# Prompt attention of one inference step: the turn of a unit moved from two to three units behind its scores, with a third buffer of probabilities

## The chip, the core and the metric

The kernel runs on one core of one Trainium2 chip. The metric is the time of one execution on the device, in microseconds (us); of several runs the median is given. The core has a matrix engine (TensorE, PE in the profile), with its weight loads shown apart as PEld, a vector engine (VectorE, DVE), an activation engine (ScalarE, ACT), GpSimd (POOL) and SyncE (SP), which issues most of the DMA transfers. Each engine works through its own list of instructions in order; engines wait for each other with semaphores.

## What is computed

One layer of a hybrid decoder for a prompt of 1024 rows and for 8 samples of 4 rows that share its weights: an RG-LRU head group, an attention group with compressed, selected and window branches, and a feed-forward block. The change touches only the selected and the window branch of the prompt. Cut to what matters (8 heads of 64, 2 key heads, 4 query heads to each key head):

```python
def sel_attend(q, q_pos, idx, valid, kg, vg):      # selected: with 1024 rows, all 16 blocks of 64 keys up to the query
    s = jnp.einsum('bqkgd,bqknld->bqkgnl', qg, kg).astype(jnp.float32) * ATTN_SCALE
    s = jnp.where(m, s, NEG_INF).reshape(B, Sq, N_KV_HEADS, GROUP, n_sel * SEL_BLOCK)
    p = jax.nn.softmax(s, axis=-1).astype(q.dtype)
    o = jnp.einsum('bqkgm,bqkmd->bqkgd', p, vg.reshape(...))

def window_prompt(q, kv):                          # window: the last 512 keys, in blocks of 128 queries
    s = jnp.einsum('bnqkgd,bnskd->bnkgqs', qb, band[:, :, :, 0]).astype(jnp.float32) * ATTN_SCALE
    p = jax.nn.softmax(jnp.where(m, s, NEG_INF), axis=-1).astype(q.dtype)
    o = jnp.einsum('bnkgqs,bnskd->bnqkgd', p, band[:, :, :, 1])

attn = g[:, :, 0] * o_c + g[:, :, 1] * o_s + g[:, :, 2] * o_w     # the gates of the three branches
```

Everything is in float32. The new keys and values are outputs too, so the tile kvn that holds them is stored to memory.

## The kernel before

The stages follow one another as blocks: input projection with the recurrent group, keys and values, compression of the blocks of keys, prompt attention, sample attention, and the trunk with output projection and feed-forward. The block of the prompt attention is the function prompt_attention.

Its work is cut into N = 128 units, listed in `order`: for each of four passes i (KA = 4, a query head of each key head), for each of 8 query tiles t of 128 rows, for the branch br (1 selected, 2 window), for each key head h. So a pass has PER = 32 units, and a unit's number in its pass is u = 4t + 2(br - 1) + h. A unit attends to w key tiles of 128: t + 1 tiles in the selected branch, at most 5 in the window branch. What is done for unit n:

- qk(n), L1458 to L1481 on PE: scores into PSUM, in two products (L1475, L1477) for a high and a low part of the queries, and a mask product (L1480). Scores of odd and even units have halves of their own (place), so qk(n) waits for the exponential of n - 2.
- top(n), L1657 on DVE: the maximum of each row, once the scores are there.
- exp(n), L1562 on ACT: exponential out of PSUM into probs[n % 2], with the row sums (a second instruction that reads the accumulator).
- weigh(n), L1674 and L1675 on DVE: reciprocal of the sum, then probabilities times reciprocal and gate, in place.
- turn(n), on PE: transposes of each 128x128 tile of the probabilities, the first four into PSUM bank 4 (L1490), the others into bank 5 (L1497). It waits for weigh(n), for the copy of the unit before out of bank 4, and in its second half for the copy out of bank 5. Units with w over 4 (`second`) have a second half: those of tiles t = 4 to 7.
- copy(n), on ACT for bank 4 (L1570) and on DVE for bank 5 (L1666), into pT[n % 4].
- weighted(v), on PE: for the pair of units 2v and 2v + 1, which are the two key heads, the product of the transposed probabilities with the values (L1516), summed over both branches in one bank, behind the compressed branch's product (L1508). take(v) on ACT (L1578) copies the finished tile.

Each engine's order is written out by hand as a loop over the iteration n. PE: qk(n), turn(n - 2), at some u a piece of the compressed branch, and at even n weighted((n - 4) // 2). ACT: copy(n - 2), exp(n), pieces, at odd n a take. DVE: top(n), weigh(n - 1), copy(n - 2), pieces. These pieces belong to the next pass: the compressed branch's scores on PE at u = 3 (L1447), shifted on DVE at u = 4 (compress_shift, L1630 to L1634, and pick_gates, L1623), their exponential on ACT, weighing on DVE at u = 6, transposes on PE at u = 9 and their copy on DVE at u = 10; and the split of the queries into high and low part (stage, L1615 and L1618 on DVE, double, L1551 on ACT), one half at u = 19 for the next pass and the other at u = 3 for the running one.

Where buffers lie: probs[0] and probs[1] in `space`; pT[0] and pT[1] in kT, whose transposed keys are dead once split into KS; pT[2] and pT[3] in the columns of kvn that held the compressed branch's keys and values. kvn's columns 256 to 384 hold the selected keys, which the loop doesn't read, but which are an output. The stores of kvn's rows (semaphore kv_stored) are issued in the stage of keys and values; SP waits for them at the end of this block.

Of the kernel before, what the change touches and what calls it, by code (L numbers as in the profile page):

```python
# [27 lines left out]
ACT = mybir.ActivationFunctionType  # L28
# [4 lines left out]
P = 128  # L33
D_MODEL = 1024
SEQ = 1024
DEC_BATCH = 8
# [9 lines left out]
KV_WIDTH = N_KV * HEAD_DIM  # L46
# [19 lines left out]
TILES = SEQ // P  # L66
# [1237 lines left out]
def prompt_attention(k, q_plain, q_rot, qT, qR, kvn, kT, gates, ck_p, cv_p, attnT, attn_sum, ident, ones, kv_stored, scratch_stored,  # L1304
# [7 lines left out]
    nc, ps, psum, d = k.nc, k.ps, k.psum, k.dram  # L1312
# [8 lines left out]
    order = [(i, t, br, h) for i in range(KA) for t in range(TILES) for br in (1, 2) for h in range(N_KV)]  # L1321
# [16 lines left out]
    with ExitStack() as st:  # L1338
# [4 lines left out]
        def take_space(n):  # L1343
            nonlocal at
            at += n
            return space[:, at - n:at]
        cmask = take_space(TILES * NBP).rearrange("p (t n) -> p t n", t=TILES)
        vx = take_space(4 * P).rearrange("p (x n) -> p x n", x=4)
        probs = [take_space(SEQ), take_space(SEQ)]
        acc = take_space(SEQ)  # L1350
        diag, tail = probs[0][:, 0:P], probs[0][:, P:2 * P]
        flat_kT = kT[:, :, :].rearrange("p a n -> p (a n)")
        pT = [flat_kT[:, p * SEQ:(p + 1) * SEQ].rearrange("p (j n) -> p j n", j=TILES) for p in range(2)] + [
            kvn[:, 0:TILES, p * P:(p + 1) * P] for p in range(2)]
        own = [slice(h * HEAD_DIM, (h + 1) * HEAD_DIM) for h in range(N_KV)]
        KS = [sb(nc, st, f"k_halves{h}", [P, 2, SEQ], F32R) for h in range(N_KV)]
# [83 lines left out]
        def _(pe):  # L1440
# [43 lines left out]
            def turn(n):  # L1484
                pe.wait_ge(scaled, n + 1)
                w = len(tiles_of[n])
                if n >= 1:
                    pe.wait_ge(copied0, n)
                for j in range(min(w, 4)):
                    m = pe.transpose(ps[4][:, j * P:(j + 1) * P], probs[n % 2][:, j * P:(j + 1) * P], ident[:, :])  # L1490
                m.then_inc(turned0, 1)
                if second[n]:
                    if upto[n] >= 2:
                        pe.wait_ge(copied1, upto[n] - 1)
                    pe.wait_ge(cmp_copied, min(trip_of(n)[0] + 2, KA))
                    for j in range(4, w):
                        m = pe.transpose(ps[5][:, (j - 4) * P:(j - 3) * P], probs[n % 2][:, j * P:(j + 1) * P], ident[:, :])  # L1497
                    m.then_inc(turned1, 1)

            def weighted(v):  # L1500

                i, t, br, _ = order[2 * v]
                bank = ps[6 + t % 2]
                if br == 1:
                    if v >= 4:
                        pe.wait_ge(taken, (v // 2 - 1) * N_KV)
                    pe.wait_ge(cmp_copied, i + 1)
                    pe.matmul(bank[:, 0:P], lhsT=vx[:, t % 4, :], rhs=cT[i % 2][:, t // 4, :], start=True, stop=False, skip_group_check=True)  # L1508
                pe.wait_ge(copied0, 2 * v + 2)
                if second[2 * v + 1]:  # L1510
                    pe.wait_ge(copied1, upto[2 * v + 1])
                tiles = tiles_of[2 * v]
                for j, kt in enumerate(tiles):
                    for h in range(N_KV):
                        col = 2 * KV_WIDTH * br + KV_WIDTH + h * HEAD_DIM
                        m = pe.matmul(bank[own[h], 0:P], lhsT=kvn[:, kt, col:col + HEAD_DIM], rhs=pT[(2 * v + h) % 4][:, j, :],  # L1516
                                      start=False, stop=(br == 2 and j == len(tiles) - 1), skip_group_check=True)
                m.then_inc(out_summed, 1)
# [8 lines left out]
            for n in range(2, DONE):  # L1527
                i, u = trip_of(n)
                if n < N:
                    qk(n)  # L1530
                if 0 <= n - 2 < N:
                    turn(n - 2)
                if i + 1 < KA:
                    if u == CMP_AT:
                        compress_scores(i + 1)
                    if u == TURN_AT:
                        compress_turn(i + 1)
                if n % 2 == 0 and n >= 4:
                    weighted((n - 4) // 2)
            for t in range(TILES):  # L1540
                pe.wait_ge(squared, t + 1)
                m = pe.matmul(ps[4][:, 2 * t:2 * t + 2], lhsT=acc[:, t * P:(t + 1) * P], rhs=ones[:, 0:2], start=True, stop=True)
# [2 lines left out]
        @block.scalar  # L1545
        def _(act):
            def double(i, half):
                cols = slice(half * HQ, (half + 1) * HQ)
                for h in range(N_KV):
                    act.wait_ge(q_hi_done, (i * 2 + half) * N_KV + h + 1)  # L1550
                    act.activation(QD[h][own[1 - h], cols], QD[h][own[h], cols].bitcast(F32), ACT.Copy).then_inc(q_doubled, 1)  # L1551

            def exp(n):
                act.wait_ge(max_ready, n + 1)
                if n >= 2:
                    act.wait_ge(turned0, n - 1)
                    if second[n - 2]:
                        act.wait_ge(turned1, upto[n - 2])
                w = len(tiles_of[n]) * P
                if n >= 4:  # L1560
                    act.wait_ge(scaled, n - 3)
                act.activation(probs[n % 2][:, 0:w], psum[:, place[n]:place[n] + w], ACT.Exp,  # L1562
                               bias=nmax[:, n % 4:n % 4 + 1], accum_out=den[:, n % 4:n % 4 + 1]).then_inc(probs_ready, 1)

            def copy(n):
                act.wait_ge(turned0, n + 1)
                if n >= 4:
                    act.wait_ge(out_summed, (n - 4) // 2 + 1)
                w = min(len(tiles_of[n]), 4)
                act.activation(pT[n % 4][:, 0:w, :], ps[4][:, 0:w * P].rearrange("p (j n) -> p j n", j=w), ACT.Copy).then_inc(copied0, 1)  # L1570

            def take(v):

                i, t, _, _ = order[2 * v]
                act.wait_ge(out_summed, v + 1)
                for h in range(N_KV):
                    head = i + h * GROUP
                    act.activation(attnT[own[head % 2], head // 2, t * P:(t + 1) * P], ps[6 + t % 2][own[h], 0:P], ACT.Copy  # L1578
                                   ).then_inc(taken, 1)

            def compress_exp(i):
                act.wait_ge(cmp_shifted, i + 1)
                act.activation(cs[:, :, :, :], cs[:, :, :, :], ACT.Exp).then_inc(cmp_exp, 1)

            for h in range(N_KV):
                split_hi(act, KS[h][own[h], :, :], kT[own[h], :, 0:SEQ]).then_inc(k_hi_done, 1)
            double(0, 0)
            compress_exp(0)
            double(0, 1)
            for n in range(DONE + 1):  # L1590
                i, u = trip_of(n)
                if 0 <= n - 2 < N:
                    copy(n - 2)
                if n < N:
                    exp(n)
                if n < N and u == EXP_AT and i + 1 < KA:
                    compress_exp(i + 1)
                if n < N and u == FIRST_HALF_AT and i + 1 < KA:
                    double(i + 1, 0)
                if n < N and u == SECOND_HALF_AT and i:  # L1600
                    double(i, 1)
                if n % 2 == 1 and n >= 5 and order[n - 5][2] == 2:
                    take((n - 5) // 2)

        @block.vector
        def _(dve):
# [62 lines left out]
            def weigh(n):  # L1669
                i, t, br, h = order[n]  # L1670
                j = slice(n % 4, n % 4 + 1)
                w = len(tiles_of[n]) * P
                dve.wait_ge(probs_ready, n + 1)
                s.then(dve.reciprocal(coef[:, j], den[:, j]))  # L1674
                dve.tensor_scalar(probs[n % 2][:, 0:w], probs[n % 2][:, 0:w], coef[:, j], gsel[i % 2][:, t, br, h:h + 1],  # L1675
                                  ALU.mult, ALU.mult).then_inc(scaled, 1)

            s.then(dve.memset(ck_pair[:, :, :], 0.0))
# [18 lines left out]
            for n in range(1, DONE):  # L1697
                i, u = trip_of(n)
                if n < N:
                    top(n)  # L1700
                if n - 1 < N:
                    weigh(n - 1)
                if 0 <= n - 2 < N:
                    copy(n - 2)
                if i + 1 < KA:
                    if u == SHIFT_AT:
                        compress_shift(i + 1)
                        pick_gates(i + 1)
                    if u == PROBS_AT:
                        compress_weigh(i + 1)  # L1710
                    if u == COPY_AT:
                        compress_copy(i + 1)
                    if u == FIRST_HALF_AT:
                        stage(i + 1, 0)
                if 0 < i < KA and u == SECOND_HALF_AT:
                    stage(i, 1)
# [1258 lines left out]
```

## Time and profile before

| what | before |
|---|---|
| three runs | 1849.24, 1849.65, 1858.37 us; median 1849.65 |
| the profiled execution | 1851.05 us, of which the span of the page is 1849.3 us |
| PE busy | 1686.2 us (91%) |
| weight loads (PEld) busy | 1490.7 us (81%) |
| DVE busy | 946.8 us (51%) |
| ACT busy | 755.9 us (41%) |
| POOL busy | 333.2 us (18%) |
| the loop of the prompt attention | about 545 to 836 us |
| granted clock, mean over the span | 0.946 |

Times in rows are us from the start of the span. In a row of the timeline come start, duration, engine, line, operation, the tile written and those read, shapes, and in brackets the idle time of this engine before it, with the work that ended it. The page names tiles by the memory they lie in: probs and attnT are shown as hT, PSUM as banks, pT as kT or kvn. A stretch's row has for each engine the busy time and the count of instructions, then the granted PE clock (1 is 2.4 GHz, 0.5 is 1.2 GHz), the DMA share and GB/s.

### The profile page before, as it was taken

The numbers are of one execution on the slowest core, as the hardware profiler recorded it, in microseconds if no ns is written. First come the engines' busy times: TensorE is split into PE (matmuls) and PEld (weight loads), VectorE is DVE, ScalarE is ACT, GpSimd is POOL, SyncE is SP. The second block draws the span as 40 slices with busy tenths as digits, with TensorE's granted clock in tenths as the row PEclk, the third lists the DMA queues.
The fourth block names the chain that finished last, engine by engine and source line by source line (L and its number), as shares of the span: only waits on it lengthen the run. The fifth ranks groups of instructions, "written<-read, shape, count | busy, mean of one in ns | idle before, by whom it ended". The sixth has DMA issues, their size and how long they took to land. (4 is left out here: it accounts for less than half of the span.)

```text
span 1849.3 us, 29408 instructions
## 1 busy us (share of the span) xinstructions
PE 1686.2 (91%) x11059; PEld 1490.7 (81%) x11059; DVE 946.8 (51%) x1611; ACT 755.9 (41%) x1233; POOL 333.2 (18%) x359
## 2 busy tenths in 40 slices
PE   6999979889968888897679979999999999999998
PEld 3888945468856676674469979999999999999997
DVE  3747662335457777674466624443444443444433
ACT  3435501134436666661233435432335432355322
POOL 1100042411020010011036404004205014100032
PEclk7999989978869999998889989999999999999999
DMA  8345320155300000104534544444544545545443
GB/s 292 105 148 171 99 74 23 47 172 179 119 6 1 1 2 1 52 2 194 230 102 136 170 151 133 137 117 132 159 136 136 152 118 148 143 130 159 123 141 94
DMA packets 297019, 214.38 MB, mean 116 GB/s; under 512 B 20365, under 2 KB 284349, under 8 KB 293662
## 3 DMA queue, kind: packets, MB, share of 16 engines
q1 hardware_dynamic: 290268, 172.34, 31.7%
q0 software_dynamic: 4816, 40.73, 5.9%
q8 instruction: 60, 0.98, 0.2%
q10 hardware_dynamic: 1842, 0.05, 0.1%
q14 instruction: 33, 0.27, 0.0%
HBM read 205.81 MB, written 11.41 MB: 117 GB/s over the span
## 5 line engine op out<-in xcount | busy, mean ns | idle before, releaser
L423 DVE TENSOR_TENSOR ff_lo<-ff_raw,ff_hi 128x2048 fp32r<-128x2048 f32 (+1 forms) x126 | 267.1, 2120 | 213.3 <-ACT ff_hi L419 213.0
L428 PE MATMUL banks<-low_rows,ff_hi 128*128 128x352 f32 x1120 | 359.6, 321 | 0.0
L427 PE MATMUL banks<-ff_h_hi,ff_hi 128*128 128x352 f32 x1056 | 342.6, 324 | 12.5 <-DVE ff_lo L423 12.5
L429 PE MATMUL banks<-ff_h_hi,ff_lo 128*128 128x352 f32 x1056 | 339.2, 321 | 0.0
L419 ACT ACTIVATE ff_hi<-ff_raw 128x2048 fp32r<-128x2048 f32 (+1 forms) x126 | 215.4, 1710 | 230.9 <-PE banks L429 225.1
L428 PEld LDWEIGHTS banks<-low_rows,ff_hi 128*128 128x128 f32 x1120 | 211.5, 189 | 0.3
L427 PEld LDWEIGHTS banks<-ff_h_hi,ff_hi 128*128 128x128 f32 x1056 | 198.7, 188 | 13.7 <-issue 13.5
L429 PEld LDWEIGHTS banks<-ff_h_hi,ff_lo 128*128 128x128 f32 x1056 | 198.4, 188 | 0.0
L427 PE MATMUL banks<-hid_hi,ff_hi 128*128 128x352 f32 x528 | 171.9, 326 | 4.4 <-DVE hid_lo L423 4.1
L429 PE MATMUL banks<-hid_hi,ff_lo 128*128 128x352 f32 x528 | 169.9, 322 | 0.0
L428 PE MATMUL banks<-hid_lo,ff_hi 128*128 128x352 f32 x528 | 169.8, 322 | 0.0
L419 ACT ACTIVATE hid_hi<-streams 128x352 f32 (+1 forms) x66 | 32.9, 498 | 232.7 <-DVE streams L2629 232.7
L1657 DVE TENSOR_REDUCE neg_max<-banks 128x1 f32<-128x640 f32 (+7 forms) x128 | 90.2, 704 | 70.0 <-PE banks L1480 69.7
L1250 DVE COPY zt<-banks 64x256 f32<-64x256 f32 (+1 forms) x192 | 66.1, 344 | 81.0 <-PE banks L1195 77.8
L2629 DVE TENSOR_TENSOR streams<-streams,banks 128x352 f32<-128x352 f32 x66 | 34.4, 521 | 139.8 <-PE banks L429 139.7
L1490 PE MATMUL banks<-ident_m,hT 128*128 128x128 f32 x416 | 73.6, 291 | 34.7 <-DVE hT L1675 33.2
L427 PEld LDWEIGHTS banks<-hid_hi,ff_hi 128*128 128x128 f32 x528 | 99.6, 189 | 5.4 <-issue 3.7
L427 PE MATMUL banks<-h_hi,s_hi 128*128 128x352 f32 x288 | 101.8, 354 | 1.6 <-DVE h_lo L423 1.1
L1208 PE MATMUL banks<-zt,w 128*128 128x256 f32 (+1 forms) x384 | 97.3, 380 | 4.9 <-DVE zt L1250 4.1
L428 PEld LDWEIGHTS banks<-hid_lo,ff_hi 128*128 128x128 f32 x528 | 99.8, 189 | 0.0
L429 PEld LDWEIGHTS banks<-hid_hi,ff_lo 128*128 128x128 f32 x528 | 99.5, 188 | 0.0
L928 PE MATMUL banks<-w_nat,hT 128*128 128x396 f32 (+1 forms) x288 | 98.6, 502 | 0.0
(425 smaller groups left out, 3136.6 us busy)
## 6 DMA issues: line engine op xcount, KB each, us to landing
ff_raw<-in_w_gate SPq DMA_DIRECT2D x66, 512.0 KB, 3.9
ff_raw<-in_w_up SPq DMA_DIRECT2D x66, 512.0 KB, 5.1
ff_raw<-in_w_down SPq DMA_DIRECT2D x48, 384.0 KB, 3.9
late_ada<-in_w_ada SPq DMA_DIRECT2D x16, 1024.0 KB, 5.4
ff_raw<-in_w_down SPq DMA_DIRECT2D x48, 320.0 KB, 3.2
ff_raw<-in_w_out SPq DMA_DIRECT2D x24, 512.0 KB, 4.7
s_raw<-in_w_in SPq DMA_DIRECT2D x48, 128.0 KB, 2.4
streams<-in_x_prompt SPq DMA_DIRECT2D x4, 1024.0 KB, 8.9
```

What stands on the lines that cost most here:

```text
L419: return act.activation(hi, raw, ACT.Copy)
L423: return dve.tensor_tensor(lo, raw, hi.bitcast(F32), ALU.subtract)
L427: pe.matmul(out, lhsT=w_hi, rhs=x_hi, start=first, stop=False)
L428: pe.matmul(out, lhsT=w_hi, rhs=x_lo, start=False, stop=False)
L429: return pe.matmul(out, lhsT=w_lo, rhs=x_hi, start=False, stop=last)
L928: m = pe.matmul(ps[2 * (t % 2) + h][0:n, 0:HN], lhsT=hT[:, c, t * P:t * P + n], rhs=w[:, c, h * HN:(h + 1) * HN], start=(c == 0), stop=(c ...
L1208: m = pe.matmul(sums(g, c), lhsT=w1[p][:, c, l, :], rhs=zt[at % 2][:, c, 0:n], start=False, stop=False, skip_group_check=True)
L1250: copy(zt[at % 2][e * HEAD_DIM:(e + 1) * HEAD_DIM, :, h * n:(h + 1) * n], ps[4 + 2 * (at % 2) + e][h * HEAD_DIM:(h + 1) * HEAD_DIM, 0:2 * ...
L1490: m = pe.transpose(ps[4][:, j * P:(j + 1) * P], probs[n % 2][:, j * P:(j + 1) * P], ident[:, :])
L1657: dve.tensor_reduce(nmax[:, n % 4:n % 4 + 1], psum[:, place[n]:place[n] + w], AX, ALU.max, negate=True).then_inc(max_ready, 1)
L2629: dve.tensor_tensor(silu[p], silu[p], ps[2 * (1 - p) + 1][:, 0:GR], ALU.mult).then_inc(mixed, 1)
```

## The change

The turn of a unit comes one unit later, and what hangs on it too. A third buffer of probabilities takes the first 1024 columns of kT; the turned probabilities that lay there go to kvn's columns 256 to 384. On PE, turn(n - 3) stands behind qk(n), and weighted((n - 5) // 2) behind it at odd n. On ACT and DVE copy(n - 3) takes the place of copy(n - 2); exp(n) waits for the turn of n - 3 instead of n - 2; take moves on by one iteration. As the turned probabilities of unit 0 now overwrite selected keys of kvn, copy(0) on ACT waits until kvn is stored. DVE's order of top(n), weigh(n - 1) and the pieces stays. The whole diff:

```diff
--- before.py
+++ after.py
@@ -1346,11 +1346,11 @@
             return space[:, at - n:at]
         cmask = take_space(TILES * NBP).rearrange("p (t n) -> p t n", t=TILES)
         vx = take_space(4 * P).rearrange("p (x n) -> p x n", x=4)
-        probs = [take_space(SEQ), take_space(SEQ)]
+        flat_kT = kT[:, :, :].rearrange("p a n -> p (a n)")
+        probs = [take_space(SEQ), take_space(SEQ), flat_kT[:, 0:SEQ]]
         acc = take_space(SEQ)
         diag, tail = probs[0][:, 0:P], probs[0][:, P:2 * P]
-        flat_kT = kT[:, :, :].rearrange("p a n -> p (a n)")
-        pT = [flat_kT[:, p * SEQ:(p + 1) * SEQ].rearrange("p (j n) -> p j n", j=TILES) for p in range(2)] + [
+        pT = [kvn[:, 0:TILES, 2 * KV_WIDTH:2 * KV_WIDTH + P], flat_kT[:, SEQ:2 * SEQ].rearrange("p (j n) -> p j n", j=TILES)] + [
             kvn[:, 0:TILES, p * P:(p + 1) * P] for p in range(2)]
         own = [slice(h * HEAD_DIM, (h + 1) * HEAD_DIM) for h in range(N_KV)]
         KS = [sb(nc, st, f"k_halves{h}", [P, 2, SEQ], F32R) for h in range(N_KV)]
@@ -1487,14 +1487,14 @@
                 if n >= 1:
                     pe.wait_ge(copied0, n)
                 for j in range(min(w, 4)):
-                    m = pe.transpose(ps[4][:, j * P:(j + 1) * P], probs[n % 2][:, j * P:(j + 1) * P], ident[:, :])
+                    m = pe.transpose(ps[4][:, j * P:(j + 1) * P], probs[n % 3][:, j * P:(j + 1) * P], ident[:, :])
                 m.then_inc(turned0, 1)
                 if second[n]:
                     if upto[n] >= 2:
                         pe.wait_ge(copied1, upto[n] - 1)
                     pe.wait_ge(cmp_copied, min(trip_of(n)[0] + 2, KA))
                     for j in range(4, w):
-                        m = pe.transpose(ps[5][:, (j - 4) * P:(j - 3) * P], probs[n % 2][:, j * P:(j + 1) * P], ident[:, :])
+                        m = pe.transpose(ps[5][:, (j - 4) * P:(j - 3) * P], probs[n % 3][:, j * P:(j + 1) * P], ident[:, :])
                     m.then_inc(turned1, 1)
 
             def weighted(v):
@@ -1528,15 +1528,15 @@
                 i, u = trip_of(n)
                 if n < N:
                     qk(n)
-                if 0 <= n - 2 < N:
-                    turn(n - 2)
+                if 0 <= n - 3 < N:
+                    turn(n - 3)
                 if i + 1 < KA:
                     if u == CMP_AT:
                         compress_scores(i + 1)
                     if u == TURN_AT:
                         compress_turn(i + 1)
-                if n % 2 == 0 and n >= 4:
-                    weighted((n - 4) // 2)
+                if n % 2 == 1 and n >= 5:
+                    weighted((n - 5) // 2)
             for t in range(TILES):
                 pe.wait_ge(squared, t + 1)
                 m = pe.matmul(ps[4][:, 2 * t:2 * t + 2], lhsT=acc[:, t * P:(t + 1) * P], rhs=ones[:, 0:2], start=True, stop=True)
@@ -1552,18 +1552,20 @@
 
             def exp(n):
                 act.wait_ge(max_ready, n + 1)
-                if n >= 2:
-                    act.wait_ge(turned0, n - 1)
-                    if second[n - 2]:
-                        act.wait_ge(turned1, upto[n - 2])
+                if n >= 3:
+                    act.wait_ge(turned0, n - 2)
+                    if second[n - 3]:
+                        act.wait_ge(turned1, upto[n - 3])
                 w = len(tiles_of[n]) * P
                 if n >= 4:
                     act.wait_ge(scaled, n - 3)
-                act.activation(probs[n % 2][:, 0:w], psum[:, place[n]:place[n] + w], ACT.Exp,
+                act.activation(probs[n % 3][:, 0:w], psum[:, place[n]:place[n] + w], ACT.Exp,
                                bias=nmax[:, n % 4:n % 4 + 1], accum_out=den[:, n % 4:n % 4 + 1]).then_inc(probs_ready, 1)
 
             def copy(n):
                 act.wait_ge(turned0, n + 1)
+                if n == 0:
+                    act.wait_ge(kv_stored, 16 * (4 + DEC_BATCH))
                 if n >= 4:
                     act.wait_ge(out_summed, (n - 4) // 2 + 1)
                 w = min(len(tiles_of[n]), 4)
@@ -1589,8 +1591,8 @@
             double(0, 1)
             for n in range(DONE + 1):
                 i, u = trip_of(n)
-                if 0 <= n - 2 < N:
-                    copy(n - 2)
+                if 0 <= n - 3 < N:
+                    copy(n - 3)
                 if n < N:
                     exp(n)
                 if n < N and u == EXP_AT and i + 1 < KA:
@@ -1599,8 +1601,8 @@
                     double(i + 1, 0)
                 if n < N and u == SECOND_HALF_AT and i:
                     double(i, 1)
-                if n % 2 == 1 and n >= 5 and order[n - 5][2] == 2:
-                    take((n - 5) // 2)
+                if n % 2 == 0 and n >= 6 and order[n - 6][2] == 2:
+                    take((n - 6) // 2)
 
         @block.vector
         def _(dve):
@@ -1672,7 +1674,7 @@
                 w = len(tiles_of[n]) * P
                 dve.wait_ge(probs_ready, n + 1)
                 s.then(dve.reciprocal(coef[:, j], den[:, j]))
-                dve.tensor_scalar(probs[n % 2][:, 0:w], probs[n % 2][:, 0:w], coef[:, j], gsel[i % 2][:, t, br, h:h + 1],
+                dve.tensor_scalar(probs[n % 3][:, 0:w], probs[n % 3][:, 0:w], coef[:, j], gsel[i % 2][:, t, br, h:h + 1],
                                   ALU.mult, ALU.mult).then_inc(scaled, 1)
 
             s.then(dve.memset(ck_pair[:, :, :], 0.0))
@@ -1700,8 +1702,8 @@
                     top(n)
                 if n - 1 < N:
                     weigh(n - 1)
-                if 0 <= n - 2 < N:
-                    copy(n - 2)
+                if 0 <= n - 3 < N:
+                    copy(n - 3)
                 if i + 1 < KA:
                     if u == SHIFT_AT:
                         compress_shift(i + 1)
```

## Rows read from the trace of the kernel before

**Rows 1.** The page, busy time of each engine over the span

```profile
PE 1686.2 (91%) x11059; PEld 1490.7 (81%) x11059; DVE 946.8 (51%) x1611; ACT 755.9 (41%) x1233; POOL 333.2 (18%) x359
```

**Rows 2.** Busy time by stretch, the second and the fourth pass

```profile
618.00:690.00 72.00, 63.12 (x561) 49.77 (x561) 54.09 (x132) 46.38 (x117) 9.66 (x21) 0.95 0.00 1
...
763.00:836.00 73.00, 64.31 (x586) 50.22 (x582) 48.86 (x116) 45.06 (x114) 12.89 (x28) 0.95 0.10 34
```

**Rows 3.** Waits, 545 to 840: who waited for whom, us in total, times, longest

```profile
PEld banks L1490 <- DVE hT L1675: 42.8, 59, 2.1
...
PEld banks L1475 <- ACT hT L1562: 2.2, 10, 0.3
...
PEld banks L1497 <- DVE kT L1666: 0.7, 4, 0.2
```

**Rows 4.** Timeline, second pass, tiles t = 2 and 3

```profile
635.78 0.31 PEld L1490 LDWEIGHTS banks<-ident_m,hT 128*128 128x128 f32 x3 [0.42 <-DVE hT L1675]
...
641.85 0.69 ACT L1562 ACTIVATE hT<-banks,neg_max 128x512 f32<-128x512 f32 x1
...
643.21 0.60 ACT L1570 ACTIVATE kT<-banks 128x512 f32<-128x512 f32 x1 [0.59 <-PE banks L1490]
...
646.15 0.42 PEld L1490 LDWEIGHTS banks<-ident_m,hT 128*128 128x128 f32 x4 [0.48 <-DVE hT L1675]
```

**Rows 5.** Timeline, second pass, first wait of t = 4, then tile t = 7

```profile
650.55 0.42 PEld L1490 LDWEIGHTS banks<-ident_m,hT 128*128 128x128 f32 x4 [0.55 <-DVE hT L1675]
...
680.02 0.61 PE L1490 MATMUL banks<-ident_m,hT 128*128 128x128 f32 x4
680.22 1.23 DVE L1657 TENSOR_REDUCE neg_max<-banks 128x1 f32<-128x1024 f32 x1 [1.48 <-PE banks L1480]
...
680.49 0.39 PE L1475 MATMUL banks<-k_halves,q_doubled 128*128 128x320 f32 x1
...
682.28 0.28 DVE L1666 COPY kvn<-banks 128x128 f32<-128x128 f32 x1
682.42 0.42 PEld L1490 LDWEIGHTS banks<-ident_m,hT 128*128 128x128 f32 x4 [1.04 <-DVE hT L1675]
...
682.48 0.82 DVE L1657 TENSOR_REDUCE neg_max<-banks 128x1 f32<-128x640 f32 x1
...
683.40 0.81 DVE L1675 TENSOR_SCALAR hT<-hT,coef,gate_pair 128x1024 f32<-128x1024 f32 x1
...
684.69 0.41 PE L1475 MATMUL banks<-k_halves,q_doubled 128*128 128x320 f32 x1
...
685.57 0.60 PE L1490 MATMUL banks<-ident_m,hT 128*128 128x128 f32 x4
...
687.37 0.42 PEld L1490 LDWEIGHTS banks<-ident_m,hT 128*128 128x128 f32 x4 [0.58 <-DVE hT L1675]
```

**Rows 6.** Timeline, second pass, tiles t = 0 and 1

```profile
619.32 0.14 PEld L1490 LDWEIGHTS banks<-ident_m,hT 128*128 128x128 f32 x1 [0.47 <-DVE hT L1675]
...
621.35 1.87 PE L1447 MATMUL banks<-ck_pair,streams 128*128 128x32 f32 x16
...
625.49 0.14 PEld L1490 LDWEIGHTS banks<-ident_m,hT 128*128 128x128 f32 x1 [0.80 <-DVE hT L1675]
...
627.10 0.42 DVE L1657 TENSOR_REDUCE neg_max<-banks 128x1 f32<-128x256 f32 x1
...
628.10 0.29 PEld L1490 LDWEIGHTS banks<-ident_m,hT 128*128 128x128 f32 x2 [2.11 <-DVE hT L1675]
```

**Rows 7.** Timeline, second pass, split of the next queries at u = 19

```profile
655.01 0.86 DVE L1615 TENSOR_SCALAR q_doubled<-streams 64x512 fp32r<-64x512 f32 x2
...
657.34 0.96 DVE L1657 TENSOR_REDUCE neg_max<-banks 128x1 f32<-128x768 f32 x1
...
659.28 0.42 PEld L1490 LDWEIGHTS banks<-ident_m,hT 128*128 128x128 f32 x4 [1.27 <-DVE hT L1675]
```

**Rows 8.** Busy time by stretch, behind the longest wait of the second pass

```profile
627.90:634.70 6.80, 6.60 (x32) 4.66 (x33) 4.30 (x16) 3.40 (x13) 1.38 (x3) 0.51 0.00 0
```

## What the change was expected to do

> **What bounds the kernel now.** I read the page first: TensorE (PE) is busy 1686.2 of 1849.3 us [rows 1]. The change touches only the block of the prompt attention, so the next view is busy time by stretch. The block's loop runs from about 545 to 836 us in four passes of 73 us, one for each head pair. In the second, 618 to 690, PE is busy 63.1 of 72 us, VectorE (DVE) 54.1 and ScalarE (ACT) 46.4; the others look the same [rows 2]. So PE is nearest to a bound, with some 9 us idle in each pass, and what can be won here is that idle time, some 36 us in four passes, 2% of the kernel. The view of waits says whose it is: the weight loads of the transposes at L1490 stand 42.8 us idle for the weighed probabilities (L1675), while Q, the scores, wait for an exponential 2.2 us, and the second transposes (L1497) for the copy of their bank 0.7 us [rows 3]. One wait is nearly all of it.
>
> I write Q(n) for the scores of unit n, M for its maximum, E for its exponential, W for reciprocal and weighing, T and T1 for the transposes into bank 4 and bank 5, C (ACT) and C1 (DVE) for the copies out of these, V for the weighted sum of a pair. A unit's number u is within its pass; t = u // 4 is its query tile.
>
> The timeline shows the wait's form. V stands behind every second T. Where it stands between T(n-1) and T(n), W(n) has time. Where it doesn't, PE has one T and one Q of work, while DVE must do M(n+1) first and W(n) after it, since its queue has them in that order. At t = 7 M(29) starts at 680.22 and takes 1.23, so T(28) waits 1.04 us until 682.42 [rows 5]. PE's own row beside it shows 0.90; the 0.14 between them is the overlap of one instruction with the next that a wait costs as well, so I count in weight-load idle. In the second pass there are four such waits at t = 2 and 3, from 0.42 to 0.48, in sum 2.1 us [rows 4]; eight at t = 4 to 7, from 0.55 to 0.58, in sum 5.4 us [rows 5], of which the longest, 1.27 us, is where DVE splits the next half of queries [rows 7]; and at t = 0 and 1 two of 0.80 and 2.11 us around the compressed branch's scores [rows 6], and one of 0.47. That is 10.9 a pass; 42.8 / 4 = 10.7 agrees.
>
> **The change part by part.** No instruction is added or dropped, and the shapes are the same; moving one turn buffer to the dead selected keys costs nothing by the rows, as copies into either place (kT or kvn) take 0.60 us at 512 columns; the one into kT is in [rows 4].
>
> *The wait on W.* T(n-3) behind Q(n) needs W(n-3), which DVE finished a unit earlier. All 42.8 us of this wait go. What is late next is worked out for each part of a pass.
>
> *The second bank.* T1(n-3) needs C1(n-4), and C1(n-4) stands on DVE behind M(n-1) and W(n-2). Before, the wait in T for W hid this, since C1 follows directly behind W. Take the gap without a V that begins at the end of Q(30). DVE: M 0.82 starts 0.03 later; from 682.48 to the end of W at 684.21 it takes 1.73, a one-tile C1 (0.28, starting 0.08 before W's end) 0.20 more, and PE starts 0.06 after: 2.0 us. PE: T and T1 of five tiles 0.47 (680.02 to 680.49), starting 0.17 before Q's end, Q(31) 0.88 (684.69 to 685.57), four transposes 0.4 (by the five in 0.47): 1.6 us [rows 5]. So T1(28) waits some 0.4 us where T(28) waited 1.04. In the same way, from the same kinds of rows: T1(20) 0.2, T1(22) 0.4, T1(24) 0.25, T1(26) 0.45, T1(30) 0.3, where wider units lengthen M, W and C1 as much as Q. At the stage at u = 19 it is worse: DVE does M(19), W(18), C1(16), then the split of 2.3 us (655.01 to 657.34), M(20), W(19), and only then C1(17), at 6.0 us from the end of Q(19) [rows 7]; PE comes to T1(18) at 4.0, as it has T, V, Q, T, Q, T of work until then: 2.0 us of wait, where T(19) waited 1.27. With 0.14 for each of seven waits that makes 5.0 us instead of 5.4 in passes 0 to 2: nearly the whole gain of t = 4 to 7 turns into another wait, and 0.4 is left. The last pass has no such stage: 2.8 instead of some 4.2, 1.4 won. Sum 2.6 us.
>
> *Tiles 2 and 3.* No second bank there, so the 2.1 us go, unless ACT takes over: a pair at t = 3 costs it two C of 0.60, two E of 0.69 and 0.2 each, about 2.9 us with half a take [rows 4], against PE's 3.0; at t = 2 both stand at 2.3. I leave 0.4 for that: 1.7 a pass, 6.8 us.
>
> *Tiles 0 and 1.* The compressed scores take PE 1.87 us (L1447), and DVE shifts them ahead of M(5), which starts at 627.10, and T(4) waits for W(4) until 628.10 [rows 6]. After the change T(4) is a step later, but Q(7) stands in front of it, and needs E(5), ready at 628.1 too. So PE stops there still, some 2.0 us. What is won: V of the last pair (1.3 us) moves behind the compressed scores, where PE would only run towards this stop, less T(4) and V of the next pair (0.9) that come behind it, and 0.5 as DVE's split is over before M(4): 0.9, with the wait of 0.5 that goes, 1.4 us. I take 0.6 in pass 0, which has no last pair, and 1.4 in the others: 4.8 us.
>
> *The added wait*, kv_stored in C(0) on ACT: all of exp and copy would queue behind it. The passes show a DMA share of 0.00 to 0.01 and 1 GB/s [rows 2], so no such store is open then: nothing. The later last iteration costs nothing on PE, the work in it being the same: 0 to 0.5 us.
>
> *Sum:* 2.6 + 6.8 + 4.8 = 14.2 us, say 14.5 with rounding of the small waits. The profiled execution took 1851.05 us for a span of 1849.3; less 14.5 is 1836.6. The median shown is 1.4 below the profiled one, so 1835.2 us.
>
> **The clock, unknown in both directions.** In passes 1 to 3 the granted clock falls to 1.2 GHz for some 6.8 us behind the stop at t = 1; in 627.9 to 634.7 PE is busy 6.60 of 6.80 us [rows 8]. At 2.4 GHz this is 3.3 us of work: up to 3.3 a pass, 10 us, if the fall doesn't come. My stop of 2.0 is no longer one of two (0.80, then 2.11) but alone; against it there is a new stop of 2.0 at the stage at u = 19, where 1.27 brought no fall. I set one against the other and take 0. The Trainium skill ("TensorE: Matmul & The Clock Gate", section "HAM oscillation — how this bites in real kernels") has it that idle gaps throw the array back to the low clock and that dense work keeps it warm; by that alone the change would gain the 10 us as well. The trace agrees that the falls stand behind the longest stops, but some of these stay.
>
> **The rivals.**
> 1. *Forecast* (0.50): turn's wait goes, C1's takes half its place; 1835, own range 1828 to 1842.
> 2. *All of it is won* (0.20): DVE, freed of nothing but order, brings C1 in time, as 0.7 us of such waits in the trace now would suggest, and the stops at t = 1 shrink: 14.5 + 17 of C1's waits (3 x 5.0 + 2.8) = 32: 1818; or the clock stays up with my other terms, 10 more: 1825. Against it: DVE's order of M, W, C1 is fixed.
> 3. *It does hardly what it says* (0.20): the stop at the stage throws the clock down in three passes, 3.3 us each; 14.5 - 10 = 4.5: 1845. Or ACT is the bound at t = 1 to 3, and 7 us fall away.
> 4. *Slower* (0.10): W(n-1) waits for E(n-1), because ACT does the three-steps-old C first, which waits for T behind Q. Then M, W and C1 all shift, and each of the 28 gaps without V at t = 4 to 7 costs 1 us more: +28 - 14.5 = +13.5: 1863. It decides from the point where E(n-1) ends later than M(n). After the end of Q(n-1), E comes behind 0.3 of T, a C of 0.60 and its own 0.8 and 0.2 [rows 4, 5], so it ends at some 2.1; M(n) ends at some 3.1 even where no V lies between (T, T1 and Q 1.35, then DVE's C1 and M behind its own queue): 1 us short of it.
>
> **How the numbers follow.** A measurement of this kernel tells about 0.5%, 9.2 us, from no change: faster is under 1840.4. Forecast: 0.42 of its 0.50 under it; rival 2 wholly: 0.62. Same: 0.08, rival 3 with 0.18 and a little of 4: 0.29. Slower 0.09. The range holds the forecast, most of 2 and of 3: 1820 to 1848.
>
> **What would show it.** In the profile of the changed kernel L1490's wait for L1675 is near zero; L1497's wait for L1666 is 10 to 18 us with the longest, about 2 us, where the queries are split; Q at L1475 waits for L1562 about 2 us in each pass at t = 1; a pass takes about 69.5 instead of 73 us. If the waits at L1497 are small, rival 2 holds; if the clock is low after the stage, rival 3; if L1674 waits for L1562 in every unit, rival 4. The prediction is wrong, too, if the block after this one gives the time back, which reads nothing of it but its end.

## The result

The kernel after the change takes 1837.8 us (median of seven runs, 1829.3 to 1839.1) against 1850.0 us (seven runs, 1849.2 to 1858.4): a ratio of the means of 0.992, 95% interval 0.9898 to 0.9941. (Ratios here are of means; by the medians the gain is 12.2 us, by the means 14.8.) The forecast was 1835.2 us, with 1820 to 1848 as its range. The profiled execution took 1836.37 us for a span of 1834.1; the one before had 1849.3, so 15.2 us are gone from the span.

First the waits, 545 to 840 us of the kernel before in [rows 3], here 540 to 832 of the kernel after (columns: who waited for whom, us in total, times, longest). Lines have moved by two: weighing is L1677, the copies L1572 (ACT) and L1668 (DVE).

```profile
PEld banks L1497 <- DVE kT L1668: 9.3, 12, 1.6
...
PE banks L1490 <- ACT kvn L1572: 4.8, 5, 1.9
PEld banks L1497 <- DVE kvn L1668: 4.3, 12, 0.4
PEld banks L1475 <- ACT hT L1562: 3.8, 11, 1.1
PEld banks L1490 <- DVE hT L1677: 3.8, 5, 1.9
...
PEld banks L1490 <- DVE kT L1677: 2.5, 2, 2.1
```

Turn's wait for the weighing was 42.8 us in 59 places. Now 6.3 us are put down to it, in seven places, and the PE rows put 4.8 us of turn's waits down to ACT's copy out of bank 4; and the second transposes, L1497, wait 9.3 + 4.3 = 13.6 us in 24 places for the copy of their bank, where they waited 0.7. The place at u = 19, 1.27 us before [rows 7], shows it whole (timeline of after, DVE and PEld):

```profile
649.91 0.86 DVE L1617 TENSOR_SCALAR q_doubled<-streams 64x512 fp32r<-64x512 f32 x2
650.80 1.41 DVE L1620 SCALAR_TENSOR_TENSOR q_lo<-streams,q_doubled 64x512 fp32r<-64x512 f32 x2
652.24 0.96 DVE L1659 TENSOR_REDUCE neg_max<-banks 128x1 f32<-128x768 f32 x1
653.22 0.16 DVE L1676 RECIPROCAL coef<-den 128x1 f32<-128x1 f32 x1
653.42 0.61 DVE L1677 TENSOR_SCALAR hT<-hT,coef,gate_pair 128x640 f32<-128x640 f32 x1
653.95 0.29 DVE L1668 COPY kT<-banks 128x128 f32<-128x128 f32 x1
...
652.23 0.42 PEld L1490 LDWEIGHTS banks<-ident_m,kT 128*128 128x128 f32 x4 [0.33 <-issue]
654.29 0.14 PEld L1497 LDWEIGHTS banks<-ident_m,kT 128*128 128x128 f32 x1 [1.64 <-DVE kT L1668]
```

The first four transposes of unit 18 run at 652.23; the fifth waits until 654.29, 0.05 us behind the copy that frees its bank, and this copy of 0.29 us stands behind a split of 2.3 us, a maximum and a weighing that have nothing to do with it.

Where the time went, by tiles. Differences of the starts of the scores in the two timelines give, in us for each pass:

| | t = 0, 1 | t = 2, 3 | t = 4 to 7 |
|---|---|---|---|
| before, passes 0 to 3 | 17.7, 16.8, 16.0, 15.1 | 14.1, 14.6, 15.9, 14.2 | 41.4, 41.5, 41.4, 49.7 |
| after | 18.0, 15.6, 16.5, 12.9 | 13.6, 15.0, 13.4, 11.6 | 39.8, 39.8, 39.8, 47.8 |
| won | 2.6 | 5.1 | 6.8 |

The last value of each row of t = 4 to 7 reaches to the sums at the block's end. That is 14.4 us in all; the block also begins 0.6 us earlier; what follows the block takes 1010.5 us after and 1010.7 before. The tiles at t = 4 to 7, second pass, once more as stretches, before and then after (columns as in [rows 2]):

```profile
644.92:686.37 41.45, 37.24 (x353) 30.27 (x352) 32.22 (x66) 27.28 (x59) 5.52 (x12) 1.00 0.01 2
```

```profile
641.75:681.52 39.77, 37.11 (x348) 29.51 (x346) 31.96 (x66) 27.81 (x60) 6.32 (x12) 1.00 0.01 2
```

PE, DVE and ACT are as busy as before at the same clock; only idle time went, some 1.6 us of the 4.2 that PE had.

The clock has a part in the rest. In the profiled execution after, the low stretch behind the stop at t = 1 is still there in the second and third pass, but no longer in the last. These are t = 0 to 3 of the second and last pass, after:

```profile
611.16:641.75 30.59, 27.19 (x222) 20.65 (x220) 22.05 (x68) 18.60 (x58) 2.66 (x6) 0.89 0.00 1
...
751.25:775.75 24.50, 22.62 (x204) 16.71 (x203) 18.77 (x56) 18.08 (x57) 3.73 (x8) 1.00 0.26 98
```

The last pass, whose t = 0 to 3 took 29.3 us before at a granted clock of 0.88, takes 24.5 at 1.00. The first pass pays for it: the low stretch in which the loop begins ends at 556.1 us before and at 562.3 after. The stretch from 556 to 562 us, before and then after:

```profile
556.00:562.00 6.00, 4.17 (x34) 2.91 (x34) 4.74 (x18) 3.88 (x14) 0.00 (x0) 0.99 0.00 1
```

```profile
556.00:562.00 6.00, 6.00 (x29) 4.29 (x31) 4.89 (x17) 3.95 (x14) 0.00 (x0) 0.50 0.00 1
```

Within the block the stretches at 1.2 GHz add up to 36.1 us in either trace. So the clock by itself explains nothing of the 14.4 us; it took from the first pass what it gave to the last.

### The profile page after: what moved, and what is told of

Same layout as the page of the kernel before. It is cut to its first block and busy times, and to the rows that moved or that the text cites. A ratio compares the mean times of both kernels' runs of the same rounds, so it can differ in the third digit from the quotient of the medians.

```text
span 1834.1 us, 29407 instructions
## 1 busy us (share of the span) xinstructions
PE 1692.5 (92%) x11059; PEld 1494.6 (81%) x11059; DVE 946.9 (52%) x1611; ACT 756.8 (41%) x1233; POOL 334.3 (18%) x359
## 5 line engine op out<-in xcount | busy, mean ns | idle before, releaser
L427 PEld LDWEIGHTS banks<-ff_h_hi,ff_hi 128*128 128x128 f32 x1056 | 198.6, 188 | 13.6 <-issue 13.3
L1259 ACT ACTIVATE zt<-banks 64x256 f32<-64x256 f32 (+1 forms) x192 | 60.8, 317 | 92.2 <-PE banks L1195 89.6
```

The source lines that it names most:

```text
L427: pe.matmul(out, lhsT=w_hi, rhs=x_hi, start=first, stop=False)
L1259: copy_turn(act, lambda o, x: act.activation(o, x, ACT.Copy), copied_a, 1, i, p, v)
```

## The experiments

Theory O: PE waited because DVE's list puts a maximum before the weighing that turn needs; one unit more of distance takes that wait away, and the copy of bank 5, which stands last in the same list, waits in its place. Rivals: the third buffer by itself (B); that PE has nothing left to give, the chain over the exponential being next (P); the clock alone, which the 36.1 us at 1.2 GHz in both traces speak against.

**The third buffer alone.**

```diff
-                if 0 <= n - 3 < N:
-                    turn(n - 3)
+                if 0 <= n - 2 < N:
+                    turn(n - 2)
```

with weighted, both copies and take back at their old distances; the buffers' places and the wait for kv_stored stay as changed.

> The changed kernel with its third buffer, its new places and its wait for kv_stored, but the turn, the copies and the weighted sums again where they were (n-2). Theory O (the order of turn against DVE's maximum and weighing makes the gain, the buffer only allows it): same time as before, 1850 us within 2, the waits of L1490 for the weighing again about 43 us. Rival B (exponentials waited for the turn that empties their buffer): most of the 12 us gain is here, about 1840. If kv_stored costs anything, it shows as more than 1852.

Measured: 1852.3 us, 1852.0 for the kernel before beside it, ratio 0.9998 (0.9981 to 1.0016). The waits:

```profile
PEld banks L1490 <- DVE hT L1677: 29.5, 40, 2.1
...
PEld banks L1490 <- DVE kT L1677: 13.2, 19, 2.1
```

29.5 + 13.2 = 42.7 us in 59 places, as before. The buffer, the new places and the wait on the stores show no gain and no cost, within 0.2%; B falls. Even the low stretches of the clock fall in the same four places as before, which suggests that they follow the order of work and are not only chance.

**The other way to the same wait: weighing ahead of the maximum.** The kernel before, with one swap on DVE:

```diff
                 if n < N:
-                    top(n)
+                    pass
                 if n - 1 < N:
                     weigh(n - 1)
+                if n < N:
+                    top(n)
```

> The kernel before with one swap in DVE's list: weigh(n-1) ahead of top(n); turn stays at n-2 and there are two buffers. Theory O says that turn waits because weighing stands behind the maximum of the unit after it; the swap then shortens the waits of L1490 from 43 to below 25 us, but each maximum now waits for the exponential of the unit before, so that part comes back as waits of L1475 for L1562: between 1840 and 1858 us. Rival D (distance alone counts, the order in DVE's list doesn't): L1490 keeps 35 us or more of waits and the time stays within 3 us of 1850.

Measured: 1873.2 us, ratio 1.0124 (1.0095 to 1.0152): slower by 21 to 23 us, outside of what I had expected.

```profile
PEld banks L1475 <- ACT hT L1562: 23.2, 49, 0.9
...
PEld banks L1497 <- DVE kT L1666: 12.8, 23, 0.9
PEld banks L1497 <- DVE kvn L1666: 10.6, 15, 0.9
PEld banks L1490 <- DVE hT L1675: 10.1, 18, 1.3
```

Turn's wait falls from 42.8 to 10.1 us, so it was the order in DVE's list that made it, and rival D, for which only distance counts, is wrong. But a maximum behind a weighing waits for the exponential of the unit before, and now the scores wait 23.2 us for exponentials. The term that I had left out is the third: 23.4 us at L1497. The copy of bank 5 stands behind the maximum and moves back with it. These three waits make 56.7 us where they made 45.7, and that is 11 of the 21 to 23 us; where the rest comes from isn't shown in full. The block was also at 1.2 GHz for 42.9 us instead of 36.1.

**The copy of bank 5 ahead of the weighing.** The kernel after, with

```diff
+                if 0 <= n - 3 < N:
+                    copy(n - 3)
                 if n - 1 < N:
                     weigh(n - 1)
-                if 0 <= n - 3 < N:
-                    copy(n - 3)
```

> The changed kernel with DVE's copy of bank 5, copy(n-3), ahead of weigh(n-1). Theory O: the waits of the second transposes (L1497) that took the place of turn's, 13.6 us in the changed kernel's trace, fall below 3 us, and the kernel gains 8 to 12 us on the changed one: 1826 to 1830. Rival P (PE has no such reserve; the loop is bound by the chain scores, maximum, exponential, scores): L1497's waits turn into waits of L1475 for L1562, and the time stays at 1835 to 1839.

Measured: 1824.2 us, ratio 0.9859 (0.9835 to 0.9883); by the means 26 us less than the kernel before, where the change alone has 15. The median is below the 1826 to 1830 that I had expected. L1497's waits:

```profile
PEld banks L1497 <- DVE kT L1668: 2.4, 3, 0.8
```

Its three places are those behind the split at u = 19. A pass takes 36.9 us at t = 4 to 7 in each of the passes 0 to 2, where the kernel after took 39.8 and the one before 41.4. So both parts of theory O hold: the waits were what held these tiles, and PE had the reserve. P falls; it is busy 36.22 of 37.12 us in this stretch, which begins 0.2 us before the tiles:

```profile
638.95:676.07 37.12, 36.22 (x352) 29.63 (x348) 31.87 (x66) 27.84 (x61) 6.08 (x12) 1.00 0.01 2
```

**The same edit without the change**, on the kernel before (copy(n - 2) ahead of weigh(n - 1)).

> The kernel before (turn at n-2) with DVE's copy of bank 5 ahead of weigh(n-1). Theory O: at n-2 turn waits for the weighing itself, and copy(n-2) ahead of it would wait for the second transposes of n-2 and put the weighing off further, so nothing is won: 1850 to 1862, waits of L1490 for the weighing 43 us or more. Rival C (the copy's place is worth its 14 us by itself, whatever turn's distance): 1836 to 1840.

Measured: 1857.8 us, ratio 1.0033 (1.0016 to 1.005), slower by 6 us.

```profile
PEld banks L1490 <- DVE hT L1675: 52.2, 64, 2.1
```

At a distance of two the copy delays the very weighing that turn waits for: 52.2 us instead of 42.8 (540 to 860, the whole block in both). At a distance of three it delays one that nobody waits for yet. The copy's place is worth 11 us only on top of the change.

**The compressed branch's DVE pieces later.** The kernel after, with

```diff
-    CMP_AT, SHIFT_AT, EXP_AT, PROBS_AT, TURN_AT, COPY_AT = 3, 4, 4, 6, 9, 10
+    CMP_AT, SHIFT_AT, EXP_AT, PROBS_AT, TURN_AT, COPY_AT = 3, 6, 6, 8, 11, 12
```

> The changed kernel with the compressed branch's DVE pieces later: shift at u=6 instead of 4, weighing at 8, transposes at 11, copy at 12. Theory O with the stop at t=1 as worked out (maximum of unit 5 behind split and shift): the waits at t=0 and 1 in passes 0 to 2, now 2.4, 3.8 and 2.8 us in weight-load idle, halve, and the low-clock stretch behind them goes in some passes: 3 to 8 us gained on the changed kernel, 1830 to 1835. Rival S: the stop only moves two units on, as the shift still stands before a maximum: same as the changed kernel within 2 us, 1836 to 1840.

Measured: 1830.9 us, ratio 0.9896 (0.9868 to 0.9924), within what theory O had said. Tiles t = 0 to 3, second pass:

```profile
611.48:639.43 27.95, 24.75 (x222) 18.87 (x221) 21.96 (x68) 18.61 (x58) 2.62 (x6) 1.00 0.01 1
```

27.95 us at a clock of 1.00, where the kernel after took 30.59 at 0.89. The idle time of PE is hardly less, 3.20 us against 3.40, so nearly all of the 2.6 us is work done at the higher clock. Rival S is right on where the idle time went: in the second pass it falls from 2.42 to 0.60 us at t = 0 and 1, and grows from 0.97 to 2.59 at t = 2 and 3. It is cut in smaller pieces, the longest stop being 1.24 us instead of 1.81, and the low stretch is gone in the second and third pass. That the smaller pieces are what keeps the clock up is argued, not shown.

**The kernel after once more.**

> The changed kernel once more, beside the others of this call on one chip. 1835 to 1839, ratio 0.991 to 0.993.

Measured: 1837.5 us, ratio 0.992 (0.9904 to 0.9936). Its profiled execution is one of its slower ones, 1840.1 us. The clock falls in other places:

```profile
655.80:659.20 3.40, 3.40 (x23) 2.67 (x19) 0.86 (x3) 0.59 (x3) 0.78 (x2) 0.59 0.01 2
```

Here the clock fell behind the 1.65 us stop at u = 19 of the second pass as well, and the tile t = 5 took 12.4 us where it took 10.9 in the other execution. On the other hand the third pass is without its low stretch in this execution. In sum its block, from the first scores to the first product of the sums (L1542), takes 280.2 us, 0.7 less than in the other execution. What makes this one longer lies mostly behind the block: 1017.4 us from there to the end at a mean granted clock of 0.96, against 1013.3 at 0.97. In the twelve profiles this part, which no edit touches, varies from 1012.2 to 1017.4 us, so small differences are better read from the block.

**Both edits together**, and again beside the last experiment.

> The changed kernel with both edits: copy(n-3) ahead of weigh(n-1), and the compressed branch's DVE pieces later. Theory O: the two remaining terms are separate (waits at the second transposes at t = 4 to 7, stop at t = 1 with its low clock), so the gains add: 14 + 7 us on the changed kernel's 1838, so 1815 to 1819. Rival N (the next bound, PE's own work or the chain over the exponential, takes part of it): 1820 to 1826.

> The kernel e6 again, beside e8 on one chip, to compare the two: 1816 to 1823 us, ratio 0.981 to 0.985 to the kernel before.

Measured: 1821.1 us, ratio 0.9828 (0.9809 to 0.9846), and 1820.5 us, 0.9839 (0.9813 to 0.9865). In parts of the kernel before: the change 0.80%, the copy 0.61% more, the pieces 0.24% more; in sum 1.65%, and 1.61 and 1.72% were measured. By the absolute times both medians miss what theory O had said, 1815 to 1819, and lie where N had them, 1820 to 1826: I had taken 14 and 7 us from medians, where the means give 11.3 and 4.4. With intervals of some 4 us to either side the times don't decide. The block does: 280.9 us after the change, 270.6 with the copy moved, 276.1 with the later pieces, 266.4 and 266.2 with both. That is 10.3 and 4.9 us for each alone, and 14.6 for both: the two edits add up but for some 0.6 us, which is all that is left for N. This version beats both kernels, by 30 us and by about 16 us.

**The split of the queries cut in two**, high part at its place and low part two iterations later: at both places, then only at u = 19.

```diff
                     if u == FIRST_HALF_AT:
-                        stage(i + 1, 0)
+                        stage(i + 1, 0, 0)
+                    if u == FIRST_HALF_AT + 2:
+                        stage(i + 1, 0, 1)
```

> As e6, with the split of the queries cut in two on DVE: the high part at u=19 and u=3, the low part two iterations later. Theory O: what is left at u=19 is a wait of about 0.7 us in three passes, and at u=3 one of 0.5 us; both shrink: 1 to 3 us less than e6. Rival N: no difference beyond 1 us.

> As e6, with only the split at u=19 cut in two, the one at u=3 whole again. The traces of e6 and e7 say: tiles 4 to 7 take 36.9 us a pass in e6 and 36.1 to 36.5 in e7, but tiles 0 to 3 take 28.0 in e6 and 30.4 and 29.7 in e7's second and third pass, where a low-clock stretch came back. If that stretch is due to the cut at u=3 (theory O), this kernel keeps both: 0.8 us less in three passes, 2 to 3 us below e6. Rival R: where the stretch falls is chance between executions, and the median is that of e6 within 1.5 us or above.

Measured: at both places 1824.6 us, ratio 0.9852 (0.9833 to 0.9871), no gain on 0.9828 and by the medians 3 us slower, where 1 to 3 us less were expected; at u = 19 alone 1821.2 us, 0.9831 (0.9804 to 0.9858), beside 0.9839 for the version without. With the cut at both places t = 0 to 3 of the second pass took 30.46 us at 0.89, where the version without it takes 27.95 at 1.00:

```profile
608.27:638.73 30.46, 27.16 (x222) 20.82 (x221) 22.53 (x68) 18.81 (x60) 2.91 (x6) 0.89 0.01 1
```

```profile
608.93:636.88 27.95, 24.74 (x223) 18.88 (x221) 22.49 (x68) 18.90 (x60) 2.63 (x6) 1.00 0.01 1
```

The wait at u = 19 did go: t = 5 takes 9.0 to 9.4 us instead of 9.8. With the cut at u = 19 only, the tiles 4 to 7 of the three passes take 2.0 us less in sum (36.1, 36.5, 36.1 instead of 36.9 each), and the block takes 263.6 us instead of 266.2, within the 2 to 3 us that theory O had said. The median doesn't show it, the part behind the block having taken 1016.5 us there and 1012.2 in the version without. In its profile a short low stretch fell in the second pass, in that of the version without it one fell in the last.

The cut at u = 3 has a price that the PE rows show, the stop at T(5) of the second pass without it (both edits alone) and then with it:

```profile
624.53 0.41 PE L1490 MATMUL banks<-ident_m,hT 128*128 128x128 f32 x2 [1.24 <-ACT kvn L1572]
```

```profile
622.82 0.44 PE L1475 MATMUL banks<-k_halves,q_doubled 128*128 128x384 f32 x1 [0.81 <-ACT kT L1562]
...
625.13 0.66 PE L1490 MATMUL banks<-ident_m,hT 128*128 128x128 f32 x2 [1.62 <-ACT kvn L1572]
```

The low part, now at u = 5, stands ahead of M(6) on DVE; Q(8) waits 0.81 us for E(6), and the stop behind is 1.62 us long instead of 1.24, in the third pass too. Behind both of these stops the clock was low. That speaks for theory O, but as the clock also fell behind a stop of 1.23 us in the version with the cut at u = 19 only, a part of chance isn't excluded: whether the cut at u = 3 is what brings the low clock back stays open.

## Why the prediction was right, point by point

**The bound and the sum of waits** held: turn's wait went nearly whole, and the time was 2.6 us over the forecast, within the spread of the runs. The buffers' new places and the wait on the stores were costed at nothing, and the third buffer alone shows it (0.9998). A range such as "from 0.42 to 0.48" in the prediction names the first and the last of four waits; the longest of these is 0.70 us, and the sum of 2.1 us is right.

**The second bank's wait** was the step that mattered, and it came: 13.6 us against my 3 x 5.0 + 2.8 = 17.8. With the 0.14 of each, T1(20), T1(22), T1(24), T1(26) and T1(28) were put at 0.34, 0.54, 0.39, 0.59 and 0.54; in the second pass they are 0.29, 0.49, 0.36, 0.53 and 0.42 (timeline of after, the last two):

```profile
674.44 0.14 PEld L1497 LDWEIGHTS banks<-ident_m,hT 128*128 128x128 f32 x1 [0.53 <-DVE kT L1668]
...
679.69 0.42 PEld L1497 LDWEIGHTS banks<-ident_m,hT 128*128 128x128 f32 x4 [0.42 <-DVE kvn L1668]
```

T1(30), put at 0.44, doesn't wait, and T1(18), behind the split, was put at 2.14 and is 1.64. By the matmul rows PE came there 4.9 us behind the end of Q(19), put at 4.0, and went on at 6.3, put at 6.0. That makes 3.7 instead of 5.0 in the pass, and so t = 4 to 7 won 6.8 us where my sum had 2.6: this term was too small by 4.2.

**Tiles 2 and 3**, 6.8 us forecast, 5.1 measured. t = 3 alone went from 7.3 to 6.46 us in every pass, 0.84 a pass, half of the 1.7 worked out for both tiles. t = 2 carries the low clock in three of four passes, and there the time depends on where that stretch falls: 8.54 us in the second pass with it, 6.36 in the third pass of the other execution without it. (The last pass has 5.15, but lacks the compressed branch's work too.)

**Tiles 0 and 1**, 4.8 us forecast, 2.6 measured, and here the step named only the second of two causes. The stop is there and as long as said, 1.9 us, but PE doesn't stop at Q(7). It stops before it, at T(3), which waits for bank 4 (timeline of after, ACT, PE and PEld):

```profile
623.96 0.42 ACT L1585 ACTIVATE cmp_probs<-cmp_probs 128x256 f32<-128x256 f32 x1 [1.46 <-DVE cmp_probs L1636]
624.28 0.55 ACT L1580 ACTIVATE hT<-banks 64x128 f32<-64x128 f32 x2
624.86 0.28 ACT L1572 ACTIVATE kvn<-banks 128x128 f32<-128x128 f32 x1
...
625.28 0.30 PE L1490 MATMUL banks<-ident_m,kT 128*128 128x128 f32 x1 [1.81 <-ACT kvn L1572]
...
625.64 0.19 PEld L1475 LDWEIGHTS banks<-k_halves,q_doubled 128*128 128x128 f32 x1 [0.26 <-ACT hT L1562]
```

copy(2) stands on ACT behind the compressed branch's exponential, which waits 1.46 us for DVE's shift, and behind a take. I had looked at what stands ahead of the maximum on DVE, and not at what waits in ACT's list; before the change the weighing of the next unit was late as well and covered it. The weight load beside it is put down to DVE hT, 1.92: of a wait for two semaphores only the later is to be believed, and the PE row names it.

Q(7), right behind T(3), then waits for its exponential, as I had it, but only 0.26 us more. So what I had named would have held PE nearly as long by itself, as long as E(5) is no earlier; but E(5) stands behind copy(2) in ACT's list too, and ran half a us after its maximum was there (624.56). How much each is worth alone was not run.

The waiting that went is nearer to the forecast than the time. PE's idle time (stretch less busy) fell from 14.9 to 10.6 us at t = 0 and 1 over the four passes, by 4.3 where I had 4.8; at t = 2 and 3 from 7.2 to 2.2, by 5.0. Two things keep it from showing as time at t = 0 and 1. In the first pass, where the idle time fell by the 0.6 us forecast, these tiles took 0.3 us more, as the low clock lasted longer. And in the other passes T(29) of the pass before, eight transposes, now stands in u = 0, where PE is busy 0.6 us longer.

So two terms were over by 3.9 us together and one under by 4.2, and the total, 14.5 us forecast and 14.4 in the block, is much nearer than its terms. That the forecast came so near is luck.

**The clock**, set at zero from both sides: right on the whole (36.1 us at 1.2 GHz in the block before and after), wrong as a picture. In one execution the last pass lost its low stretch, and 2.2 + 2.6 us of that pass' gain at t = 0 to 3 include this, while the first pass was low for 6 us more; in another a low stretch fell behind the stop at u = 19, as rival 3 had it, and cost 1.5 us. The largest gain by the clock is that of the version with the later pieces: 1.00 instead of 0.89 over 28 us, and 2.6 us.

The Trainium skill ("TensorE: Matmul & The Clock Gate", section "HAM oscillation — how this bites in real kernels") has it as the rule that the clock stays high where the work is dense and falls behind idle gaps. The runs agree in part: the last pass of the kernel after, idle 1.9 of 24.5 us at t = 0 to 3, kept 1.00; but the version with the later pieces kept it with nearly as much idle time (3.20 us) as the kernel after, which didn't (3.40).

**Rivals.** Rival 2, that everything is won, was right in one thing: the reserve on PE is real, 36.9 us against 39.8, but the change alone doesn't reach it. Rival 4, weighing that waits for the exponential, doesn't occur after the change: such waits are 1.4 us in 5 places. Where the weighing is put ahead of the maximum, they do spread, to 83.3 us in 115 places on DVE, with the 21 to 23 us above.

**The signs.** The waits at L1497 came as said, 13.6 us with the longest 1.65 at the split. L1490's wait is not near zero, but 6.3 us by the weight loads, and the 2 us that Q at L1475 was to wait at t = 1 are nearly all spent there, ahead of Q(7). The second pass takes 70.4 us instead of 72.8, where 69.5 and 73 were named. The part behind the block gave nothing back.

## What to carry to other kernels

A wait for a step that stands late in an engine's list is a matter of the list, not of that step: see which neighbour in the list nobody waits for, and ask after each change of distance what now stands in front of what. Taking a unit more of distance between producer and consumer frees the order of the producer's list, and that second step can be worth nearly as much as the first (here 11 us after 15, by the means), while without the first it costs (6 us). A buffer or a bank that is reused every unit keeps its own wait whatever the distance: cost its release by the list of the engine that releases it, and do this for every engine that copies.

## What was not expected of the hardware

The length of a stop didn't decide whether the granted clock fell to 1.2 GHz behind it. In the second pass of the kernel after it fell behind the 1.65 us at u = 19 in one execution, and not behind 1.64 us in the other. Behind the stop at T(3) in the third pass, 1.95 us in both executions, it fell in one, just as that stop ended, and stayed at 1.00 in the other. With both edits it fell behind a stop of 1.24 us in the first pass and not behind the same stop in the second. And it also fell with no stop over 0.8 us in the 12 us before, as at 621.0 to 624.4 us in the kernel after once more, and at 749.4 to 752.8 in both edits again. So an edit that removes waiting can gain or lose with the place of such a stretch: with the split cut at u = 3 and u = 19, t = 5 took 0.4 to 0.8 us less in each of three passes, and t = 0 to 3 of the second pass 2.5 us more.
